# Scan operands turned by VectorE, silu in one ScalarE instruction, the steps behind it a unit later, and three moves in other stages

## What is computed

```python
def even_layer(...):
    proj = rms_norm(x, norm_w) @ w_in
    sc_b, sc_c, sc_v, sc_z, ssd_z, ssd_xbc, ssd_dt, mq, mz = _split(proj, EVEN_SPLITS)
    y_a = sc_b * causal_depthwise_conv(sc_c * sc_v, sc_conv_w)      # 3 taps, width 1024
    y_a = y_a * jax.nn.silu(sc_z)
    xbc = jax.nn.silu(causal_depthwise_conv(ssd_xbc, ssd_conv_w) + ssd_conv_b)  # 4 taps, 3072
    xs, bm, cm = _split(xbc, (2048, 512, 512))
    dt = jax.nn.softplus(ssd_dt + ssd_dt_bias)                      # 32 columns of proj
    y_b = ssd_chunked(xs, dt, -exp(a_log), bm, cm) + xs * ssd_d
    y_b = y_b * jax.nn.silu(ssd_z)                                  # then an rms norm per group
    return x + concatenate([y_a, y_b, y_m]) @ w_out
```

## Time and profile before

| | us |
|---|---|
| median of three runs | 2661.48 |
| the profiled execution | 2659.44 |
| its span, first to last instruction | 2657.8 |
| TensorE busy | 2635.8 |
| VectorE busy | 1564.2 |
| ScalarE busy | 1343.3 |
| GpSimd busy | 339.1 |

### The profile page before, as it was taken

How to read it: one execution, slowest core, us unless ns; L and a number is a source line. 1 busy time by engine, 2 the same in 40 slices (tenths; PEclk the granted TensorE clock), 3 DMA queues, 4 the chain that set the end, 5 groups by cost and what they waited for, 6 DMA issues and landing times. The chain is left out here.

```text
span 2657.8 us, 35526 instructions
## 1 busy us (share of the span) xinstructions
PE 2635.8 (99%) x12007; PEld 2188.8 (82%) x12007; DVE 1564.2 (59%) x1833; ACT 1343.3 (51%) x1776; POOL 339.1 (13%) x523
## 2 busy tenths in 40 slices
PE   9999999999999999999999999999999999999998
PEld 7888888888888888888888888888888789888887
DVE  6444456667555555555455665446777765556864
ACT  6544455654444444444444554446565445554443
POOL 2100032211110000000000211001110110123400
PEclk9999999999999999999999999999999999999999
DMA  8876676678776767667666887667677777787775
GB/s 311 308 228 219 214 235 217 206 239 273 230 236 215 226 207 225 209 223 227 215 219 210 264 255 232 208 203 240 223 227 228 230 251 225 227 263 230 215 234 162
DMA packets 175720, 611.77 MB, mean 230 GB/s; under 512 B 23184, under 2 KB 26304, under 8 KB 175360
## 3 DMA queue, kind: packets, MB, share of 16 engines
q1 hardware_dynamic: 133632, 485.03, 56.2%
q0 software_dynamic: 37184, 121.07, 15.5%
q10 hardware_dynamic: 4800, 4.26, 0.6%
HBM read 559.36 MB, written 52.47 MB: 230 GB/s over the span
## 5 line engine op out<-in xcount | busy, mean ns | idle before, releaser
L1859 DVE TENSOR_TENSOR w_lo<-raw,w_hi 128x1024 fp32r<-128x1024 f32 x919 | 1116.4, 1222 | 865.2 <-ACT w_hi L1283 858.5
L1283 ACT ACTIVATE w_hi<-raw 128x1024 fp32r<-128x1024 f32 x919 | 963.9, 1058 | 914.7 <-PE acc L830 769.1
L824 PE MATMUL acc<-w_hi,x_t_hi 128*128 128x512 f32 (+1 forms) x2400 | 949.9, 396 | 0.4 <-ACT w_hi L1283 0.4
L824 PE MATMUL acc<-w_hi,x_t_lo 128*128 128x512 f32 (+1 forms) x2400 | 932.9, 389 | 0.0
L830 PE MATMUL acc<-w_lo,x_t_hi 128*128 128x512 f32 (+1 forms) x2400 | 639.9, 388 | 0.6 <-DVE w_lo L1859 0.6
L830 PEld LDWEIGHTS acc<-w_lo,x_t_hi 128*128 128x128 f32 x2400 | 450.5, 188 | 93.2 <-DVE w_lo L1859 1.0
L824 PEld LDWEIGHTS acc<-w_hi,x_t_hi 128*128 128x128 f32 x2400 | 450.9, 188 | 91.8 <-issue 1.9
L824 PEld LDWEIGHTS acc<-w_hi,x_t_lo 128*128 128x128 f32 x2400 | 451.0, 188 | 90.7 <-issue 1.9
L824 PE MATMUL acc<-w_hi,ff_t_hi 128*128 128x512 f32 x352 | 136.9, 389 | 0.0
L824 PE MATMUL acc<-w_hi,ff_t_lo 128*128 128x512 f32 x352 | 136.9, 389 | 0.0
L830 PE MATMUL acc<-w_lo,ff_t_hi 128*128 128x512 f32 x352 | 94.1, 389 | 0.0
(11 more groups left out here) (395 smaller groups left out, 2677.3 us busy)
## 6 DMA issues: line engine op xcount, KB each, us to landing
raw<-stream SPq DMA_DIRECT2D x919, 512.0 KB, 4.3
d_in<-tile POOLq DMA_DIRECT2D x20, 512.0 KB, 3.7
d_ev<-tile POOLq DMA_DIRECT2D x20, 512.0 KB, 4.9
d_x<-tile POOLq DMA_DIRECT2D x16, 512.0 KB, 4.4
r_b<-d_x POOLq DMA_DIRECT2D x64, 128.0 KB, 6.4
xin<-d_x POOLq DMA_DIRECT2D x16, 512.0 KB, 7.7
d_h<-tile POOLq DMA_DIRECT2D x14, 512.0 KB, 5.7
h_b<-d_h POOLq DMA_DIRECT2D x56, 128.0 KB, 4.6
```

Source lines behind the costliest of these rows:

```text
L824: nc.tensor.matmul(out, src[x][:, chunk + c, t * P:(t + 1) * P], w_hi[:, s, w], start=first and c == 0 and x == 0, stop=False)
L1283: nc.scalar.activation(w_hi[:, u.slot, :], raw[:, u.slot, :], ACT.Copy).then_inc(hi_ready, 1)
L1859: nc.vector.tensor_tensor(w_lo[:, s, :], raw[:, s, :], w_hi[:, s, :].bitcast(F32), ALU.subtract).then_inc(lo_ready, 1)
```

## The change

- **Turned by VectorE.** `load_u` loads the six blocks with channels and tokens in 32 x 32 pieces into `u_b` (four DMAs of 32 x 8 x 192 elements a group in place of three), the host's order of the columns is changed to suit, and `turn_u` turns them with one VectorE transpose of 128 x 1536 into `u_t` in SBUF: at unit 15 of `ez` for group 0, at p = 11 of the group before for the others. TensorE's 12 transposes a group are gone, and taps read `u_t`.
- **Silu in one instruction.** `ACT.Silu` on `cv` (scale 2) and on `zt` at p = 4 replaces two tanh on ScalarE and two passes on VectorE (L2328, L2332). The factor 0.5 in L2380 is gone.
- **A unit later.** From the state's product on (p = 9 to 10, 11 to 12, 12 to 13, 13 to 14, 14 to 15) all steps of the group stand one unit later, as do `turn_group`, `high_group` and `low_group` of n < 3. `decays` for t = 0 stands at p = 15, for t = 1 at p = 1 of the next group.
- **dt.** The unit holds its 32 columns twice. `split_beside` overwrites the second copy in `w_hi` with the remainder, and 32 matmuls with 64 output rows replace the 48. Two matmuls with parts of `ident` for each half of the tokens add the two (four in place of two transposes).
- **`eout` and the short convolution.** Tap 0 goes from VectorE to ScalarE at 9j + 6, the other steps are spread out over 9j + 4 to 9j + 13, and `EOUT_ORDER` runs the second half's four units as two and two, with the wait for the second half at unit 24. Block 0 ends at unit 25 of that order and no longer at unit 23.
- **Attention.** `log_keep` of head j = 2 stands behind the split of unit 7 + 3.

```diff
-EOUT_ORDER = [(b, k) for ks in (range(10), range(10, 14)) for b in range(2) for k in ks]
+EOUT_ORDER = [(b, k) for ks in (range(10), range(10, 12), range(12, 14)) for b in range(2) for k in ks]
...
+            for b in range(P // SQ):
+                w = 1024 + 768 * g.k + 6 * SQ * b
+                pool.dma_start(u_b[b * SQ:(b + 1) * SQ, :, :],
+                               d_ev[:, w:w + 6 * SQ].rearrange("(a j) n -> j a n", j=SQ)).then_inc(s_u, 16)
...
         for c in range(16):
-            w = slice(32 * c, 32 * c + P)
-            nc.tensor.matmul(out, w_hi[:, u.slot, w], x_hi, start=c == 0, stop=False)
-            nc.tensor.matmul(out, w_lo[:, u.slot, w], x_hi, start=False, stop=False)
-            mm = nc.tensor.matmul(out, w_hi[:, u.slot, w], x_lo, start=False, stop=c == 15)
+            w = slice(64 * c, 64 * c + 64)
+            for x in range(2):
+                mm = nc.tensor.matmul(ps_y[0:64, 0:TOK], w_hi[:, u.slot, w], x3_t[x][:, c, :],
+                                      start=c == 0 and x == 0, stop=c == 15 and x == 1)
...
-            if p == 0:
-                pe.wait_ge(s_u, n.times(48, 48))
+            if p == 7:
                 pe.wait_ge(dt_v, 7)
                 pe.wait_ge(s_yb, n.times(1, 1))
-                for c in range(6):
-                    bank = (turn[0], turn[1], ps_s)[c // 2]
-                    for t in range(TH):
-                        mm = nc.tensor.transpose(...)
-                mm.then_inc(s_ut, 1)
...
-            if q in (20, 22):
-                pe.wait_ge(c_lo, q // 2 - 9)
+            if q in (20, 24):
+                pe.wait_ge(c_lo, q // 4 - 4)
...
                 splits("win", 8, 96 + 8 * b, i, 16, lambda k: attend(8 * b + k, i))
+                if b == 0:
+                    log_keep(HEAD_AT_UNIT.index(6), i)
...
+            if p == 1 and g:
+                decays(n, 1)
             if p == 3 and g:
                 open_decays(n)
             if p == 4:
                 act.wait_ge(s_conv, n.times(3, 3))
-                nc.scalar.activation(th[:, :], cv[:, :, :].rearrange("p c t -> p (c t)"), ACT.Tanh)\
-                    .then_inc(s_th, 1)
-            if p == 5:
+                c_ = cv[:, :, :].rearrange("p c t -> p (c t)")
+                nc.scalar.activation(c_, c_, ACT.Silu, scale=2.0).then_inc(s_silu, 1)
                 act.wait_ge(s_z, n.times(16, 16))
-                nc.scalar.activation(zth[:, :, :], zt[:, :, :], ACT.Tanh, scale=0.5).then_inc(s_zth, 1)
+                nc.scalar.activation(zt[:, :, :], zt[:, :, :], ACT.Silu).then_inc(s_zs, 1)
...
-            if p in (14, 15) and not last_group:
-                decays(n + 1, p - 14)
+            if p == 15 and not last_group:
+                decays(n + 1, 0)
...
+        def turn_u(g):
+
+            dve.wait_ge(s_u, 64 * (g + 1))
+            dve.wait_ge(s_conv, 3 * g)
+            nc.vector.transpose(u_t[:, :, :].rearrange("p c (a i) -> p c a i", i=SQ),
+                                u_b[:, :, :].rearrange("p a (c i) -> p c a i", i=SQ)).then_inc(s_ut, 1)
```

More of the change, by code:

```diff
@@ L209, in program @@
         ("xs", [P, TH, NBW], F32), ("xdt", [P, TH, NBW], F32), ("xde", [P, NBW], F32), ("st", [P, NBW], F32))
+    u_b = place("u_b", [P, TOK // SQ, 6 * SQ], F32, AT + 8 * K)
+    u_t = place("u_t", [P, 6, TOK], F32, END + 8 * K)
     th = place("th", [P, 6 * TOK], F32, AT + 8 * K)
@@ L1063, in time_steps @@
                 for t in range(TH):
-                    mm = nc.tensor.transpose(ps_y[:, TOK + 32 * t:TOK + 32 * t + 32], dt_t[:, t * P:(t + 1) * P],
-                                             ident[0:32, 0:32])
+                    for part in range(2):
+                        mm = nc.tensor.matmul(ps_y[:, TOK + 32 * t:TOK + 32 * t + 32], dt_t[:, t * P:(t + 1) * P],
+                                              ident[0:64, 32 * part:32 * part + 32], start=part == 0, stop=part == 1)
                 mm.then_inc(pe_once, 1)
@@ L1394, in _, with log_keep @@
                 scale_out(At(U0["win"] + 8 * b + 7, i, 16), b, At(STORED["win"], i, 1).times(16, 16), 1)
+        def log_keep(j, i):
+            J, m = At(j, i, 4), At(j // 2, i, 2)
+            act.wait_ge(at_z, J.times(1, 2))
+            nc.scalar.activation(keep[:, :], z["sb"][:, :], ACT.Abs).then_inc(at_abs, 1)
+            act.wait_ge(at_abs, m.times(1, 1))
+            nc.scalar.activation(keep[:, :], keep[:, :], ACT.Exp, scale=-1.0).then_inc(at_exp0, 1)
+            act.wait_ge(at_exp0, m.times(1, 1))
+            nc.scalar.activation(keep[:, :], keep[:, :], ACT.Ln, bias=1.0).then_inc(at_keep, 1)
         def attend(p, i):
@@ L2261, in ein_beside @@
             mem_job(0, At(0, i, 1), k - 6, z_t, At(16, i, 1).times(1))
-        for i in range(4):
+        for i in range(3):
             splits("ein", 16, 16, i, 16, lambda k: ein_beside(k, i))
+        for k in range(16):
+            ein_beside(k, 3)
+            u = At(U0["ein"] + 64 + k + LEAD)
+            if u.k == U0["dt"]:
+                split_beside(u)
+            else:
+                split(u)
         split(At(U0["dt"] + LEAD))
@@ L2360, in ssd @@
                 last.then_inc(s_m, 1)
+            if p == 10:
                 for t in range(TH):
@@ L2407, in sc_beside, with blocks_of @@
                 low_group(p, g - 1)
+            if p == 11 and g < 3:
+                turn_u(g + 1)
         for g in range(4):
             splits("sc", 16, 16 * g, 0, 0, lambda k: sc_beside(k, g))
+        def blocks_of(dst, part):
+            return nc.vector.transpose(dst[:, :, :].rearrange("p c (a i) -> p c a i", i=SQ),
+                                       sc_in[:, :, part, :].rearrange("p a (c i) -> p c a i", i=SQ))
         def short(k, j):
```

125 lines of the change are left out of this document (56 added, 69 removed).

## The result

The changed kernel takes 2648.7 us at the median of five runs (2643.0 to 2653.0), the kernel before 2661.5 us in the same job (2659.9 to 2664.2). The ratio is 0.9949, with a 95% interval from 0.9934 to 0.9964. Beside other kernels, on another occasion, the same file gave 2646.2 us and 0.9945 (0.9932 to 0.9959). So it is faster by 13 to 15 us; forecast were 13.9 us and 2647.6 us.

What follows compares the result with a forecast made beforehand. TensorE, busy 2635.8 of 2657.8 us, was taken to bound the kernel. Terms -5.3 - 1.3 - 4.0 - 0.9 - 5.2 + 2.5 + 0.3 = -13.9 us took the 2661.5 us median to 2647.6 us, range 2642 to 2654 us.

Steps and rivals of the forecast that it cites:

- Work taken from TensorE: Scan and dt unit: 12 transposes fewer in each of four groups, -5.3 us; dt with 32 matmuls for 48, -1.3 us.
- The attention's stall: Attention: with the split ahead of `log_keep`, TensorE's four waits of 0.75 us for `p_t` go, -4.0 us.
- The state's product: Scan, groups 1 to 3: a unit later `xde` is long done, so a 0.3 us gap goes in each, -0.9 us.
- The stalls in `eout`: Four stalls of TensorE in `eout` go with the short convolution's work spread over more units, -5.2 us.
- Rival 1: `eout`: the stall only moves, up to 3 us stay and block 0's turn costs 3.5 us; 2651.5 us, chance 0.17.
- Behind block 0: `eout`: block 0 ends two units later, so splits behind its turn come late at units 32 and 33, +2.5 us.
- Now the turn begins at 1.4 + 16.7 = 18.1: `eout`: add to turn stays 16.7 us as before, so unit 32's `w_lo` is done at 20.4, 2.3 us late.
- ScalarE in groups 1 to 3: Scan: decay steps and table loads lengthen ScalarE's chain, `z_t_lo` at unit 7 0.1 to 0.6 us ahead; +0.3 us.
- the second rival: Scan: each table load costs 1.4 us more, TensorE waits 7.5 us at unit 7; 2655.1 us, chance 0.06.
- Hidden: Scan: VectorE's new transpose, the `u_b` loads and the steps moved by a unit cost no time.
- signs of being wrong: Forecast is wrong if stalls of `eout` or the attention stay, or a wait for the stream shows in `sc`.
- Rival 4: Scan: small-piece `u_b` loads hold the stream, TensorE loses 16 us; slower, 2663.5 us, chance 0.02; decides from 3.5 us a group.

Runs made afterwards that it cites:

- scan_only: The kernel before with the rest of the change, without the attention's part and without `eout` and short convolution: 2654.4 us, ratio 0.9977.
- attn_only: The kernel before with only the attention's part, `log_keep` of head 2 behind the split of unit 7: 2657.6 us, ratio 0.9988.
- eout_only: The kernel before with only the new order of units in `eout` and the spread short convolution: 2655.9 us, ratio 0.9984.
- all_four_moves: The changed kernel with group 0's loads earlier, eight 128-partition loads in all groups, transpose at unit 13, block 0's turn one unit later: 2643.4 us, ratio 0.9931.

## Why group 0 of the scan stalls

**What the trace shows.** ScalarE splits three units ahead of TensorE. In unit 12 of `ez` that split found no data. The timelines of ScalarE and VectorE in the changed kernel:

```profile
1828.67 1.06 ACT L1276 ACTIVATE w_hi<-raw 128x1024 fp32r<-128x1024 f32 x1 [3.18 <-DMA raw<-stream]
...
1838.76 3.06 ACT L1629 ACTIVATE cv<-u_t,col 128x256 f32<-128x256 f32 x6 [0.89 <-DVE u_t L2323]
1841.73 3.88 ACT L1276 ACTIVATE w_hi<-raw 128x1024 fp32r<-128x1024 f32 x4
```

```profile
1835.81 1.23 DVE L1864 TENSOR_TENSOR w_lo<-raw,w_hi 128x1024 fp32r<-128x1024 f32 x1 [1.53 <-ACT w_hi L1276]
1836.95 1.77 DVE L2323 STREAM_TRANSPOSE u_t<-u_b 128x1536 f32<-128x1536 f32 x1
```

Before, the same wait was 1.67 us. Behind it stand in a row the decays, the splits, VectorE's transpose and six scaled copies, and the split at 1841.73 is the one that TensorE wants at 1841.9. Then VectorE has a pass of taps of 2.45 us and a split of 1.13 us in each unit, 3.5 us against 2.72, and three units follow before it is through. Two causes were open: the loads of `u_b` hold the stream (A), or the transpose in the row does (B).

**u_early** moves the four loads of group 0 ahead, behind the last head's work.

```diff
+        all_stored(STORED["l2"] + 4)
+        load_u(At(0))
         pool.wait_ge(dt_v, 7)
...
         all_stored(STORED["l2"] + 5)
-        load_u(At(0))
         load_z(At(0))
```

> The changed kernel with one thing moved: group 0's four loads of turned operands are issued behind the last head's work, some 25 us earlier, not between the loads of decays and of z. VectorE's transpose stays ahead of the split in unit 15 of ez. Theory A (these loads stretch the traffic of the GpSimd queue by 4 us, the stream is starved 3.2 us instead of 1.7 and ScalarE and VectorE enter the scan with no units in hand): the four stalls of group 0 go, 3.3 us less than the changed kernel, about 2645.4 us. Theory B (the transpose itself stands in a row between split, scaled copies and split): the stalls stay, within 1 us of the changed kernel.

Measured: 2643.4 us, ratio 0.9941 (0.9926 to 0.9955). ScalarE waits 1.4 us for the stream, and of the four stalls one is left (0.4 us ahead of 1845.1). The interval overlaps the changed kernel's; it is the trace that tells them apart.

**after_again** and **turn_at_13** were run beside each other.

> The changed kernel as it is, beside the three others on the same chip. 12.8 to 13.5 us less than the kernel before. If the four stalls at the start of group 0 belong to the program and not to one execution, this trace has them too, 3 to 4 us in all, and one wait for a split of 0.3 to 0.6 us behind block 0's turn.

Measured: 2646.2 us, ratio 0.9945. Two stalls of TensorE for `w_lo` are there, ahead of 1842.0 and 1845.5, not the four of 3 to 4 us that were expected, and a wait of 0.6 us for `xde`. ScalarE waits 2.6 us for the stream. In `eout` two stalls stand behind block 0's turn, for `w_lo` and for `w_hi`. So the loss in group 0 is the program's, but its size differs between executions: 3.5 us in the first, 1.2 us (0.7 us in two waits, and 0.26 each) in this one.

```diff
-            if p == 15:
+            if p == 13:
                 turn_u(0)
```

> The changed kernel with group 0's transpose on VectorE ahead of the split in unit 13 of ez, where VectorE was idle, in place of unit 15; its loads stay where they are. Theory A (the loads starve the stream): the stream is starved as before, a first stall of about 1 us goes since the scaled copies no longer wait for the transpose (0.9 us) and VectorE has 1.8 us of work less there, but most stalls stay: 1 to 2 us less than the changed kernel. Theory B (the transpose in the row between splits is the cause): all four go, 3.3 us less.

Measured: 2646.8 us, ratio 0.9941. ScalarE still waits 3.31 us for the stream, its scaled copies no longer wait for the transpose, and the trace has the same two stalls as `after_again` (0.6 us in two waits). Theory B falls as the cause of the stalls. The transpose may have a small share: the one stall that `u_early` kept is gone in both versions below that also turn at unit 13. Of A only "the stream is held by these loads" is shown so far, not why: they have the same 0.79 MB as before.

**u_wide** asked whether it is the small pieces.

```diff
-        load_u(At(0))
+        for b in range(P // SQ):
+            pool.dma_start(u_b[b * SQ:(b + 1) * SQ, :, :].rearrange("p (t c) n -> p t (c n)", t=TH),
+                           ev_v[b * SQ:(b + 1) * SQ, :, 1024:1792]).then_inc(s_u, 16)
```

> The changed kernel with group 0's turned operands loaded in pieces of 3072 bytes (256 of them) in place of 768 bytes (1024), the same 0.79 MB at the same place in the queue. The rows lie otherwise than the transpose needs, so group 0's operands are wrong numbers; nothing of the work is left out. If small pieces are what stretches the GpSimd queue (20.2 us for 2.88 MB in place of 15.6), the queue ends 4 us or more sooner, ScalarE's wait for the stream falls from 3.2 us to 1.7 or less, and at most one of the four stalls stays: 2.5 to 3.3 us less. If the bytes alone count, nothing changes.

Measured: 2646.2 us, ratio 0.9941. ScalarE waits 3.4 us for the stream, all four stalls are there, and TensorE waits 2.0 us for `xde`. Pieces four times as long change nothing. That part of theory A falls too.

**What all of these loads share** is that each DMA writes 32 partitions. The change made one load into 128 partitions (and two small ones) into four loads of 32 each. **u_all_128** takes only that away.

```diff
-        load_u(At(0))
+        for k in range(4):
+            pool.dma_start(u_b[:, 2 * k:2 * k + 2, :],
+                           ev_v[:, :, 1024 + 6 * SQ * k:1024 + 6 * SQ * (k + 1)]).then_inc(s_u, 16)
```

> The changed kernel with group 0's operands loaded by four DMAs that each write all 128 partitions, in place of four that each write 32; the pieces are again 768 bytes, 1024 of them, and the bytes, the number of DMAs and their place in the queue are the same. The rows lie otherwise than the transpose needs, so group 0's operands are wrong numbers; nothing of the work is left out. Theory C (DMAs into 32 partitions hold the chip's DMA engines back, also for the stream): while this load is under way, stream and GpSimd queue move some 400 GB/s together as in the kernel before, and not 250, ScalarE's wait for the stream falls from 3.2 us to 1.7 or less, and at most one stall of TensorE stays at the start of group 0: 2 to 3 us less than the changed kernel. 
The view that decides is the table by stretches. Each row is one stretch of 6 us that begins 8 us after the load of the decays was issued, when the operands of group 0 are on their way. The columns are busy us (and instructions) of PE, PEld, DVE, ACT and POOL, the granted clock, the DMA engines' busy share and GB/s of all queues. In this order: the kernel before, the changed kernel, u_wide, u_all_128.

```profile
1821.70:1827.70 6.00, 6.00 (x28) 4.99 (x27) 1.72 (x2) 4.33 (x13) 0.00 (x0) 1.00 1.02 401
```

```profile
1821.00:1827.00 6.00, 6.00 (x28) 4.98 (x27) 1.22 (x1) 2.87 (x9) 0.00 (x0) 1.00 1.04 233
```

```profile
1816.10:1822.10 6.00, 6.00 (x28) 4.96 (x27) 1.23 (x1) 2.89 (x9) 0.00 (x0) 1.00 1.04 231
```

```profile
1821.30:1827.30 6.00, 6.00 (x29) 4.95 (x27) 1.81 (x2) 4.64 (x13) 0.00 (x0) 1.00 1.02 401
```

The DMA engines are busy all the time in all four (share 1.0), but with DMAs into 32 partitions they move 231 to 233 GB/s and not 401. Busy says nothing about how much is moved. The stream pays its part: in the changed kernel's stretch it got some 0.6 MB, before 1.2 MB, from the packets of its queue. In `u_all_128` ScalarE waits 0.8 us for the stream, and no stall of a split stands between 1834 and 1860 us. Theory C holds on what it says of rate, wait and splits.

Two things limit these four rows. The low rate ends sooner in some executions: the same stretch has 304 GB/s in `after_again`, 263 in `turn_at_13` and 330 in `scan_only`, which all have the DMAs into 32 partitions. And every trace has a slow time ahead of the stretch, from 1816 to 1820 us in the kernel before, while the load of the decays heads GpSimd's queue, a single DMA into all 128 partitions:

```profile
1816.00:1820.00 4.00, 4.00 (x19) 3.32 (x18) 2.11 (x3) 1.72 (x2) 1.88 (x3) 1.00 1.00 231
```

So 32 partitions are not the only way to a low rate at a busy share of 1.0; the loads of `u_b` make the slow time longer. What separates the traces without overlap is ScalarE's longest wait for the stream. It is 2.6 to 3.4 us in the five that have these loads beside the decays (changed kernel, `after_again`, `scan_only`, `turn_at_13`, `u_wide`), with two to four stalls of TensorE, and 0.6 to 1.9 us in the nine others, with one stall or none.

The Trainium skill has the rule ("SBUF — State Buffer", Door 1: The DMA port swizzle): DMA bandwidth goes by the ports that the partitions reach, and 32 partitions in a row reach 8 of 16. It gives 189 against 328 GB/s for 32 and 128 partitions at 1 MiB. The trace agrees in kind, with 233 against 401 GB/s for all queues together. It is a rule against this change, and I didn't weigh it.

The time doesn't confirm the gain of 2 to 3 us: 2646.8 us, ratio 0.9947 (0.9933 to 0.9961). The trace shows one reason. Group 1's loads were left as they were, and there ScalarE waited 4.14 us for the stream, and TensorE lost 1.1 us at `xde`, ahead of 1863.9. The other is that 2 us is less than five runs tell apart.

**u_eight_loads** gives all groups loads into 128 partitions, with the right rows: one block of 32 tokens for all four column blocks in each DMA.

```diff
-            for b in range(P // SQ):
-                w = 1024 + 768 * g.k + 6 * SQ * b
-                pool.dma_start(u_b[b * SQ:(b + 1) * SQ, :, :],
-                               d_ev[:, w:w + 6 * SQ].rearrange("(a j) n -> j a n", j=SQ)).then_inc(s_u, 16)
+            for k in range(8):
+                src = bass.AP(d_ev.tensor, 1024 + 768 * g.k + k * SQ * 10240,
+                              [[6 * SQ, P // SQ], [10240, SQ], [1, 6 * SQ]])
+                pool.dma_start(u_b[:, k, :], src).then_inc(s_u, 16)
...
-            dve.wait_ge(s_u, 64 * (g + 1))
+            dve.wait_ge(s_u, 128 * (g + 1))
```

> The changed kernel with the turned operands of all four groups loaded by eight DMAs that each write all 128 partitions (one block of 32 tokens for all four column blocks), in place of four into 32 partitions. The result is computed as in the changed kernel. GpSimd issues four DMAs more a group, about 2.3 us, so the loads of z and the store behind them come that much later. Theory C: wait for the stream 1.7 us or less, at most one stall at the start of group 0, 2 to 3 us less than the changed kernel, about 2645.5 us. Rival D: no better than the changed kernel, and the later store could cost up to 1 us.

Measured: 2643.1 us, ratio 0.9936 (0.9922 to 0.9949), the 2 to 3 us below the changed kernel that were expected, though the intervals overlap. ScalarE waits 0.8 us for the stream in all, one stall of 0.5 us is left, and no wait for `xde` in group 0. One thing did not go as expected. The same stretch as above:

```profile
1815.70:1821.70 6.00, 6.00 (x28) 4.95 (x28) 1.91 (x2) 4.68 (x13) 0.00 (x0) 1.00 1.05 259
```

The rate is low here too, but the stream is spared: by the packets of the queues, it moved 236, 182 and 160 GB/s in the three thirds of this stretch, against 57, 127 and 131 in the changed kernel, and the GpSimd queue took the slowness. That holds for group 0. From 1834 to 2036 us, where the loads of the other groups fall, ScalarE waits for the stream 18.1 us in this kernel and 9.4 us in the changed one, and TensorE waits for no split in either but at the start of group 0. Why these eight are slow was not tried. The Trainium skill would have it that each of them uses 4 of 16 DMA engines ("DMA: Bandwidth & Descriptors", Why a DMA increments its semaphore by 16 and not by 1), since their source has an outermost dimension of 4; no run here shows it.

**before_quarters** puts the fault into the kernel before: two thirds of its operands go by four DMAs into 32 partitions each.

```diff
-            pool.dma_start(u_in[:, :, 0:512], ev_v[:, :, bass.ds(g.times(512, 1024), 512)]).then_inc(s_u, 16)
+            for b in range(P // SQ):
+                w = slice(b * SQ, (b + 1) * SQ)
+                pool.dma_start(u_in[w, :, 0:512], ev_v[w, :, bass.ds(g.times(512, 1024), 512)]).then_inc(s_u, 16)
...
-                pe.wait_ge(s_u, n.times(48, 48))
+                pe.wait_ge(s_u, n.times(96, 96))
```

> The kernel before with two thirds of each group's operands (0.52 of 0.79 MB) loaded by four DMAs into 32 partitions each, in place of one into 128; the data are the same. GpSimd issues three DMAs more, about 2.1 us. Theory C: the fault of the changed kernel appears in the kernel before: ScalarE's wait for the stream ahead of group 0 grows from 0.9 to 1.7 us to 2.3 us or more, with the rate of both queues falling below 300 GB/s while these loads are under way; TensorE has more units in hand here than in the changed kernel, so 0 to 1.5 us of stalls. Rival D: wait for the stream within 0.3 us of the kernel before, no time lost.

Measured: 2662.7 us, ratio 1.0004 (0.9995 to 1.0013). It falls between the two. The rate does drop, but for one slice of 2 us:

```profile
1821.60:1823.60 2.00, 2.00 (x10) 1.68 (x9) 1.23 (x1) 1.25 (x4) 0.00 (x0) 1.00 1.03 254
```

ScalarE's wait for the stream is 1.9 us, less than the 2.3 us of C and within the 0.3 us of D (1.7 us in the kernel before). The load is shorter (0.52 MB, in pieces of 2048 bytes) and in one stretch of the queue. So this run shows the lower rate, and that it does no harm when it is short; it is no second proof of the stalls.

## Versions that leave the stalls out

**early_13_turn_later** has the early load, the transpose at unit 13 and one edit more, for block 0's turn in `eout`:

```diff
-X4_AT = {(2, 1): 0, (2, 6): 1, (3, 5): 2}
+X4_AT = {(2, 2): 0, (2, 6): 1, (3, 5): 2}
```

> The changed kernel with three moves: group 0's turned operands loaded 25 us earlier, its transpose at unit 13 of ez, and block 0's turn in eout one unit later (unit 2 of block 2). The stall of 0.55 us that was left with the early load alone goes with the second, the 0.4 to 0.56 us for unit 33's split with the third, since this split then stands ahead of the scaled copies. By my sum 3.3 + 0.67 = 4.0 us less than the changed kernel, about 2644.7 us; at the least 3.0 us less.

Measured: 2643.6 us, ratio 0.9931 (0.9917 to 0.9944). Its TensorE waits for nothing from 1830 to 1860 us, and has no idle bracket from 2120 to 2130 us.

> The changed kernel with four moves together: group 0's turned operands loaded 25 us earlier, the loads of all groups by eight DMAs that write all 128 partitions each, group 0's transpose at unit 13 of ez, block 0's turn in eout one unit later. The version with the other three moves had no stall at the start of group 0 nor behind block 0's turn, and the eight loads alone had neither the stalls nor the 0.3 to 1 us wait for the state's product in group 0. So between 870 us and the end I expect no stall of TensorE but the ones of every group; in time 3.5 to 4.5 us less than the changed kernel, a ratio of 0.993 to the kernel before, and no more than 0.5 us less than the version with three moves, which a measurement can't tell.

Measured: 2643.4 us, ratio 0.9931 (0.9917 to 0.9944). The four together are no better than three, as expected. That no other stall would appear was wrong: there is one of 0.3 us for a split in group 3 at 2001 us, behind scaled copies for which VectorE had waited 2.9 us, and one of 0.2 us for `z_t_lo` at unit 7. By the ratios both versions are 3.7 us faster than `after_again` (0.9931 against 0.9945), and the intervals overlap: what tells them apart is the traces, not the times.

## Why the prediction was right, and where it was not

The number was right to about 1 us (12.8 us by the medians and 13.6 by the ratio, for 13.9), and the parts add up. But two terms were wrong, one too dear and one at nothing, and in good part they cancel. That is luck.

**Work taken from TensorE: right.** The 48 transposes are gone. The dt unit and what follows it, in the timeline of TensorE, answer to the earlier trace rows:

```profile
1784.68 0.28 PE L1056 MATMUL ps_y<-x_t_hi,w_hi 128*64 128x256 f32 x1
...
1788.32 0.40 PE L826 MATMUL acc<-w_hi,x_t_hi 128*128 128x512 f32 x1
...
1791.16 1.07 PE L1065 MATMUL ps_y<-ident,dt_t 64*128 64x32 f32 x8
1792.16 0.50 PE L826 MATMUL acc<-w_hi,x_t_hi 128*128 128x512 f32 x1
```

The unit takes 3.64 us (3.80 forecast) and the eight records 1.00 us in place of 0.24 (0.87 forecast). Net -1.3 us, as predicted, by two small errors against each other.

**The attention's stall: right.** It is gone in `attn_only` and in all four turns of the changed kernel, for 3.2 to 4.0 us. The split stands ahead of `log_keep` now, and that ends without harm.

**The state's product: right for groups 1 to 3**, where the product and what follows it take 1.33 us from the start of the matmul ahead of it to the second one behind, and 1.71 us before: 0.38 us each in place of my 0.3. A new one stands in group 0 in five of the ten traces with the new scan, and costs 0.4 us in the changed kernel, 1.1 in `u_all_128` and 2.7 in `u_wide`. In `u_all_128` it stands behind VectorE's wait for splits that waited 4.14 us for the stream, while group 1's `u_b` was being loaded.

**The stalls in `eout`: right.** All four are gone. (The taps' 1.13 + 3.37 us are 4.50 and not 4.45; nothing hangs on it.) ScalarE's longest wait for the stream there fell from 8.51 us to 3.93 us, and that no longer reaches TensorE. Rival 1 did not happen.

**Behind block 0: the term was mis-sized, 2.5 us forecast and 0.7 us in the profiled execution** (0.4 + 0.26). In the other traces with the new order it is 0.3 (`eout_only`) to 1.9 us (`u_wide`), where the `w_lo` ahead of it is late too. The mechanism is the one forecast: the split of unit 33 stands behind four scaled copies. The step that failed is "Now the turn begins at 1.4 + 16.7 = 18.1". In the timeline of VectorE it begins 15.44 us after the add. With that the prediction's own count has unit 33's `w_hi` at 15.4 + 3.9 = 19.3, 0.3 us late, and 0.40 us was measured:

```profile
2114.29 1.41 DVE L2487 SCALAR_TENSOR_TENSOR tile<-xin,rstd,acc 128x512 f32<-128x512 f32 x2 [0.34 <-PE acc L832]
...
2129.73 1.25 DVE L1906 STREAM_TRANSPOSE r_t<-r_b 128x1024 f32<-128x1024 f32 x1 [7.46 <-issue]
```

It was 17.3 to 18.1 us in the four traces with the old order, and 15.1 to 16.6 us in the eight with the new one and the turn at unit 1. DMA issues around block 0's add and turn (KB each, us to landing), before (19 us) and after (17 us):

```profile
raw<-stream SPq DMA_DIRECT2D x6, 512.0 KB, 8.2
...
r_b<-d_x POOLq DMA_DIRECT2D x4, 128.0 KB, 7.0
```

```profile
raw<-stream SPq DMA_DIRECT2D x4, 512.0 KB, 6.0
...
r_b<-d_x POOLq DMA_DIRECT2D x4, 128.0 KB, 4.3
```

Loading block 0 back takes 4.3 us in place of 7.0, with fewer loads of the stream beside it. Their number follows from the order. A slot's load waits for its `w_lo`, and between the add and the turn VectorE has five splits in the old order and three in the new one, since the add comes two units later and the turn does not. Then it waits for block 0 (7.46 us, 4.64 before), and the stream's queue waits for VectorE. The waits of that queue for `w_lo` (total, times, longest), before from 2116 to 2136 us and after from 2113 to 2134 us:

```profile
SPq L401 <- DVE w_lo L1859: 11.8, 6, 3.0
```

```profile
SPq L403 <- DVE w_lo L1864: 17.7, 5, 9.2
```

The traces of `attn_only` and `scan_only`, which have the old order, have five issues of the stream between add and turn, that of `eout_only` three. So the step took its 16.7 us from a time in which the stream ran on, and the change makes the late turn itself hold the stream back while the block is loaded. That the quieter stream is what makes the load faster is my reading of these traces; no run varied it alone.

**ScalarE in groups 1 to 3: right.** The changed kernel has no wait at unit 7. The margin is as thin as I counted (0.1 to 0.6 us): `u_early` and `all_four_moves` wait 0.2 us for `z_t_lo` once each. ScalarE has the 29 table loads that were forecast, each 1283 ns. One of them, answering to the earlier trace rows, in ScalarE's timeline:

```profile
1901.21 1.04 ACT L1276 ACTIVATE w_hi<-raw 128x1024 fp32r<-128x1024 f32 x1
1902.27 1.28 ACT L1640 ACT_TABLE_LOAD   x1
1903.57 1.49 ACT L1640 ACTIVATE cv<-cv 128x1536 f32<-128x1536 f32 x1
```

1.28 us with 0.02 us on either side, so the second rival, with 1.4 us more for each load, falls. It is so at 24 of the 29; behind the other five ScalarE waits for VectorE.

**Hidden: this step failed.** I wrote that "`u_b` has 1024 pieces of 768 bytes a group; its time to p = 11 is over four units". That held for groups 1 to 3 as far as TensorE goes, but group 0's load comes together with the decays, `z` and a store, and there it costs 1.1 to 3.5 us in the traces with it. One of my signs of being wrong did show, a wait for the stream in `sc`. ScalarE's waits for it from 1834 to 2036 us, before and after (total, times, longest):

```profile
ACT w_hi L1283 <- DMA raw<-stream: 0.3, 1, 0.3
```

```profile
ACT w_hi L1276 <- DMA raw<-stream: 9.4, 9, 3.4
```

The longest stands at 1862.0 us, behind group 1's load. TensorE waits for no split behind these nine, since ScalarE had units in hand; only ahead of group 0 did it have none left. Rival 4 had the mechanism nearly right ("If `u_b` holds the stream"), named small pieces as its cause, which `u_wide` refutes, and set against it "`u_b` is 0.79 MB and not 2.1 MB, like the load that it replaces". Bytes were the wrong measure; over which partitions each DMA writes them made the difference in group 0. It stayed far from its point of 3.5 us a group because only group 0's load cost TensorE more than the 0.4 us at `xde`.

**The accounting of the profiled executions.** The sum without its two terms for new waits is -16.7 us. Add 3.5 us for the stalls of group 0, 0.4 for `xde` there, 0.7 behind block 0, and 0.5 for the wait at 379 us; take off 0.5 for one at 2430 us that is gone. That gives -12.1 us. The other 4 us are in two stretches that the change doesn't touch. Adding up what the distances between matmuls exceed 0.227 us by, the first 14 us of the kernel have 3.0 us before and 4.9 us after, and 700 to 800 us has 2.3 and 4.5 us (there counting distances over 0.56 us). Both vary from execution to execution whatever the kernel: 2.7 to 5.4 us and 0 to 4.6 us over all fourteen traces; `before_quarters`, with the old code in both stretches, has 5.2 and 0 us. So -12.1 + 1.9 + 2.2 = -8.0 us, and 8.1 us was measured.

## What to carry to other kernels

Count the partitions that each DMA writes, not its bytes alone: with a load split into DMAs of 32 partitions all queues moved 231 to 330 GB/s in six microseconds in which they moved 401 without, and what suffered was the weight stream beside it. Place such a load where the engines fed by the stream have units in hand (`u_early`: 231 GB/s from 1785 to 1791 us, and no wait for the stream from 1780 to 1810 us), or shape it so that each DMA reaches all partitions, and then read the rate: eight such DMAs had 259 GB/s. A duration that is read from a trace holds what ran beside it. Where the change moves what an engine does while it lasts, as here two splits and the stream's loads that wait for them, count anew what will run beside it, and bound the term from a place without it.

## What the runs showed of the hardware that I had not expected

The DMA engines' busy share was 1.0 at 401 GB/s and also at 231 GB/s, with DMAs into 32 partitions and with the load of the decays into 128: busy engines are not full ones. Pieces of 768 and of 3072 bytes gave the same rate (233 and 231 GB/s) when each DMA wrote 32 partitions. And where the next ACTIVATE waits for nothing, a table load of ScalarE costs its 1.28 us and 0.02 us on either side, also in front of a Silu of 1536 columns.
